# Attention scores from high and low parts in three products, and one group of block inverses turned a stage later

## What is computed

```python
q = partial_rope(rms_norm(q, g_q)) * d ** -0.5        # (B, T, 4 heads, 2 parts, d = 64)
k = partial_rope(rms_norm(k, g_k))
s = einsum('bqhcd,bkhcd->bhcqk', q, k)                # float32 scores, c = two parts
pr = softmax(s, axis=-1)
amap = pr[:, :, 0] - lam * pr[:, :, 1]
out = einsum('bhqk,bkhe->bqhe', amap, v)              # e = 128
```

## Time and profile before

| | us |
|---|---|
| median of 3 runs (lowest to highest) | 2118.28 (2113.72 to 2121.5) |
| the profiled execution | 2117.55 |
| its span, first to last instruction | 2115.7 |
| mean granted TensorE clock in it | 0.968 |

### The profile page before, as it was taken

How to read it: one execution, slowest core, us unless ns; L and a number is a source line. 1 busy time by engine, 2 the same in 40 slices (tenths; PEclk the granted TensorE clock), 3 DMA queues, 4 the chain that set the end, 5 groups by cost and what they waited for, 6 DMA issues and landing times. The chain is left out here.

```text
span 2115.7 us, 40868 instructions
## 1 busy us (share of the span) xinstructions
PE 1958.3 (93%) x16327; PEld 1657.1 (78%) x16327; DVE 1386.8 (66%) x2230; ACT 974.9 (46%) x1854; POOL 353.4 (17%) x354
## 2 busy tenths in 40 slices
PE   5999999999767888869999799999999999999999
PEld 4666777777665666658886688999999999988887
DVE  4877757675676668667777557755655556647566
ACT  7454458785564555534454323432333322343433
POOL 0000000000007999274463100000000000000000
PEclk9999999999788999879999999999999999999999
DMA  4111147786950000148983532222222222394343
GB/s 186 67 47 46 69 179 245 243 281 222 358 196 34 1 1 1 34 116 192 204 182 108 180 120 110 90 84 91 98 84 84 84 92 102 131 340 146 100 144 112
DMA packets 151867, 275.22 MB, mean 130 GB/s; under 512 B 12960, under 2 KB 85408, under 8 KB 149504
## 3 DMA queue, kind: packets, MB, share of 16 engines
q1 hardware_dynamic: 151392, 271.27, 39.9%
q10 hardware_dynamic: 288, 1.34, 0.2%
HBM read 169.67 MB, written 99.93 MB: 127 GB/s over the span
## 5 line engine op out<-in xcount | busy, mean ns | idle before, releaser
L222 PE MATMUL normed_acc<-right_t_high,normed_lefts 128*128 128x320 f32 x528 | 163.8, 310 | 3.8 <-DVE normed_lefts L3107 3.8
L224 PE MATMUL normed_acc<-right_t_high,normed_lefts 128*128 128x320 f32 x528 | 163.8, 310 | 0.0
L223 PE MATMUL normed_acc<-right_t_low,normed_lefts 128*128 128x320 f32 x528 | 163.8, 310 | 0.0
L3107 DVE TENSOR_TENSOR normed_lefts<-held_room,normed_lefts 128x512 fp32r<-128x512 f32 x149 | 102.3, 687 | 91.1 <-ACT normed_lefts L2993 91.1
L222 PE MATMUL normed_acc<-normed_nl 128*128 128x512 f32 x385 | 149.8, 389 | 0.0
L224 PE MATMUL normed_acc<-normed_nl,normed_nh 128*128 128x512 f32 x385 | 149.8, 389 | 0.0
L2993 ACT CAST normed_lefts<-held_room 128x512 fp32r<-128x512 f32 x149 | 90.4, 620 | 109.5 <-DMA held_room<-in_w_up 48.3
L3015 ACT COPY normed_n<-normed_acc 128x640 f32<-128x640 f32 x64 | 44.5, 695 | 206.5 <-PE normed_acc L224 203.5
L3179 DVE TENSOR_TENSOR normed_nl<-held_room,normed_nh 128x640 fp32r<-128x640 f32 x77 | 63.3, 823 | 91.7 <-ACT normed_nh L3041 91.6
L3041 ACT CAST normed_nh<-held_room 128x640 fp32r<-128x640 f32 x77 | 56.1, 728 | 143.8 <-PE normed_acc L224 124.6
L222 PE MATMUL pj_acc<-parts_nh,pj_w0rest 128*128 128x512 f32 (+1 forms) x288 | 110.1, 382 | 7.1 <-DVE parts_nl L804 7.1
(11 more groups left out here) (414 smaller groups left out, 5639.0 us busy)
## 6 DMA issues: line engine op xcount, KB each, us to landing
held_room<-dram_h SPq DMA_DIRECT2D x77, 320.0 KB, 3.0
dram_sx<-pr_sx SPq DMA_DIRECT2D x16, 1024.0 KB, 4.5
ch_ops<-dram_sx SPq DMA_DIRECT2D x56, 256.0 KB, 5.2
dram_h<-held_room SPq DMA_DIRECT2D x44, 320.0 KB, 2.3
pj_packed<-in_w_in SPq DMA_DIRECT2D x24, 512.0 KB, 4.9
heads_vt<-dram_ab SPq DMA_DIRECT2D x44, 256.0 KB, 7.1
held_room<-in_w_gate SPq DMA_DIRECT2D x22, 512.0 KB, 4.4
held_room<-in_w_up SPq DMA_DIRECT2D x22, 512.0 KB, 4.4
```

What stands on the lines that cost most here:

```text
L222: nc.tensor.matmul(out, ll, rh, start=start, stop=False, skip_group_check=onto_kept)
L223: nc.tensor.matmul(out, lh, rl, start=False, stop=False, skip_group_check=onto_kept)
L224: return nc.tensor.matmul(out, lh, rh, start=False, stop=stop, skip_group_check=onto_kept)
L3107: tt(lefts[:, q % LEFTS, 1, :], raw[:, y, QUARTER[p], :], lefts[:, q % LEFTS, 0, :].bitcast(F32), ALU.subtract).then_inc(low, 1)
```

## The change

The score product is no longer one float32 matmul. Queries and keys are split into a high part (a copy into the type fp32r, by ScalarE) and a low part (what is left, subtracted by VectorE), and each score piece is the sum of three fp32r matmuls: low query with high key, high query with low key, high with high. The keys of a head are split once, in two pieces (the short sequence's 272 columns, the long one's 1040); the queries are split for each unit, two units ahead, into two buffers. For heads 1 to 3 the short piece is split in unit i = 5 of the head before, the long piece in unit i = 0. On ScalarE the copies stand at the end of a step, behind `out_of`; on VectorE the subtractions stand behind `largest(k, 1)` and ahead of `turn_inverse`, each with a wait for the copy. TensorE waits for the low parts. The tiles of the stage are laid out anew, and ScalarE waits, ahead of its step 1, for the stores of the stage before. `EARLY` goes from 4 to 3.

```diff
@@ -1020,7 +1020,7 @@
     return (n % GS // 2 * 4 + x * 2 + n % 2) * FT + f
 
 
-PAIR, EARLY = 2, 4
+PAIR, EARLY = 2, 3
 
 
 def links_until(pair):
@@ -1916,11 +1916,13 @@
     ALL = len(units)
...
+        kh, kl = (c.sb(n, (P, TOK), F32R) for n in ("kh", "kl"))
+        qh, ql = ([c.sb(f"{n}{s}", (P, P), F32R) for s in range(2)] for n in ("qh", "ql"))
+        st = [c.sb(f"st{s}", (P, 2, 4)) for s in range(2)]
+        lams = c.sb("lams", (P, 4))
         pr = [[c.sb(f"pr{s}{x}", (P, LEN_B)) for x in range(2)] for s in range(2)]
         amT = [c.sb(f"amT{s}", (P, 9, P)) for s in range(2)]
-        st = [c.sb(f"st{s}", (P, 2, 4)) for s in range(2)]
         lam = g.lam
-        lams = c.sb("lams", (P, 4))
         solve_chain, first_in = c.sem("solve_chain"), c.sem("first_in")
         FIRST_TURN = ALL - 4 * EARLY
         pS = [c.ps(f"pS{x}", (P, 3 * 512)) for x in range(2)]
...
+        k_high, k_low, q_high, q_low = (c.sem(n) for n in ("k_high", "k_low", "q_high", "q_low"))
+        KEYS = (slice(0, LEN_A), slice(LEN_A, TOK))
+        SHORT = sum(u[3] == LEN_A for u in units[:NU])
+
+        def splits_behind(k):
+
+            h, i = k // NU, k % NU
+            return [(h + 1, 0)] if i == NU // 2 and h + 1 < HEADS else [(h, 1)] if i == 0 and h else []
 
         turned, act_copied = c.sem("turned"), c.sem("act_copied")
         tiles_of = [[range(0, 4), range(4, 8), range(8, 9)] if u[3] == LEN_B else [range(0, 3)] for u in units]
@@ -1961,13 +1971,16 @@
                     if k:
                         for x in range(2):
                             pe.wait_ge(exped[x], k)
+                    pe.wait_ge(q_low, k + 1)
+                    if k % NU in (0, SHORT):
+                        pe.wait_ge(k_low, 2 * h + (1 if k % NU == 0 else 2))
                     for lo in range(0, ln, 512):
                         hi = min(lo + 512, ln)
-                        for x, rows in enumerate(HALVES):
-                            last = mm(pS[x][:, lo:hi], g.qr[rows, h, q0:q0 + P], g.kr[rows, h, a + lo:a + hi],
-                                      start=True, stop=True)
-                            if hi == ln:
-                                last.then_inc(scores[x], 1)
+                        for n, (left, right) in enumerate(((ql, kh), (qh, kl), (qh, kh))):
+                            for x, rows in enumerate(HALVES):
+                                last = mm(pS[x][:, lo:hi], left[k % 2][rows, :], right[rows, a + lo:a + hi], start=n == 0, stop=n == 2)
+                                if hi == ln and n == 2:
+                                    last.then_inc(scores[x], 1)
 
                 def turn(k, b):
                     ln = units[k][3]
@@ -2027,12 +2040,32 @@
                         last = nc.scalar.copy(amT[k % 2][0:kn, full, :], pTail[0:kn, :] if b == 2 else pT[0:kn, full * P:(full + 1) * P])
                     last.then_inc(act_copied, 1)
 
+                def high_keys(h, part):
+                    if h:
+                        for x in range(2):
+                            act.wait_ge(scores[x], NU * (h - 1) + SHORT if part == 0 else NU * h)
+                    nc.scalar.copy(kh[:, KEYS[part]], g.kr[:, h, KEYS[part]]).then_inc(k_high, 1)
+
+                def high_queries(k):
+                    if k >= 2:
+                        for x in range(2):
+                            act.wait_ge(scores[x], k - 1)
+                    q0 = units[k][1]
+                    nc.scalar.copy(qh[k % 2][:, :], g.qr[:, units[k][0], q0:q0 + P]).then_inc(q_high, 1)
+
                 def out_of(k):
                     act.wait_ge(outs, k + 1)
                     nc.scalar.copy(g.o_rows[:, units[k][0], k % NU, :], pO[:, 0:P]).then_inc(ocopied, 1)
+                high_queries(0)
+                high_keys(0, 0)
+                high_queries(1)
+                high_keys(0, 1)
                 act.wait_ge(lamb, 1)
                 nc.scalar.activation(lams[:, 0:2], lams[:, 0:2], ACT.Exp).then_inc(lamb, 1)
                 for k in range(ALL + 2):
+                    if k == 1:
+                        for sem, n in g.solve_stored:
+                            act.wait_ge(sem, n)
                     if 1 <= k <= ALL:
                         turn_copy(k - 1, 0)
                     if k < ALL:
@@ -2043,6 +2076,11 @@
                             turn_copy(k - 1, b)
                     if k >= 2:
                         out_of(k - 2)
+                    if k < ALL:
+                        for h, part in splits_behind(k):
+                            high_keys(h, part)
+                    if k + 2 < ALL:
+                        high_queries(k + 2)
 
             @block.vector
             def _(dve):
@@ -2091,6 +2129,18 @@
                         nc.vector.transpose(g.by_row_early[:, grp, :, part].rearrange("p u c -> p c u"),
                                             g.inv[:, grp, :, part].rearrange("p i j -> p j i"))
 
+                def low_keys(h, part):
+                    dve.wait_ge(k_high, 2 * h + part + 1)
+                    nc.vector.tensor_tensor(kl[:, KEYS[part]], g.kr[:, h, KEYS[part]], kh[:, KEYS[part]].bitcast(F32), ALU.subtract).then_inc(k_low, 1)
+
+                def low_queries(k):
+                    q0 = units[k][1]
+                    dve.wait_ge(q_high, k + 1)
+                    nc.vector.tensor_tensor(ql[k % 2][:, :], g.qr[:, units[k][0], q0:q0 + P], qh[k % 2][:, :].bitcast(F32), ALU.subtract).then_inc(q_low, 1)
+                low_queries(0)
+                low_keys(0, 0)
+                low_queries(1)
+                low_keys(0, 1)
                 lambda_sums()
                 for k in range(ALL + 1):
                     if k:
@@ -2100,6 +2150,11 @@
                         largest(k, 1)
                     if k == 0:
                         lambdas()
+                    if k < ALL:
+                        for h, part in splits_behind(k):
+                            low_keys(h, part)
+                    if k + 2 < ALL:
+                        low_queries(k + 2)
                     if FIRST_TURN <= k < ALL:
                         turn_inverse(k - FIRST_TURN)
 
```

## The result

The changed kernel takes 2190.72 us (median of 4 runs, 2185.67 to 2196.69), the kernel before 2117.12 beside it: ratio 1.034, interval 1.0318 to 1.0363. The forecast was 2182, its range 2155 to 2214. The profiled execution took 2187.64 us (span 2185.9, mean clock 0.955). What follows is its trace.

What follows compares the result with a forecast made beforehand. The attention stage was taken as bound by a loop of score, maxima and exponential, 5.90 us long, hiding the difference with 0.31 to spare. Terms 24.2, 17.7, 2.3, 11.5, 6 and 3.2 added 64.9 to 2117.55: 2182 us, range 2155 to 2214.

Steps and rivals of the forecast that it cites:

- the difference no longer starts at E + 0.1 but after ScalarE's whole tail: Each unit's query split: VectorE's reciprocal and difference wait for ScalarE's query copy and its subtraction, held 1.25 us.
- E: In the attention stage, the moment when both exponentials of a unit are done; VectorE's reciprocal followed 0.1 us later.
- Ordinary steps: Long units after long units: 1.05 us more each, 23 times, 24.2 us; query subtraction of 128 columns taken as 0.28.
- Short keys: Units 5, 15, 25, where 272 key columns are split: 0.77 us each, 2.3 us in all.
- Long keys: Blocks around units 10, 20, 30, where 1040 key columns are split: 5.9 us each, 17.7 in all.
- Inverses: VectorE's inverse pieces, exposed whole between query wait and difference in ten steps: 1.15 us each, 11.5 in all.
- Clock: TensorE's clock falls after idle time in steps with exposed inverses: 6 us, between 0 and 15.
- Start: Attention stage's start, first score and exponential behind the first splits: unit 3 comes 3.2 us late (2 to 5).
- in ordinary units too: Rival: TensorE's clock falls also after the 1.4 us idle time of ordinary units, 34 us more: 2212 us; chance 0.11.
- halves apart: Rival: score halves run one after the other on TensorE, scores of 2.7 to 4 us: 2194 us; chance 0.09.
- The score decides: Rival: the query split costs the loop under 0.31 us, so only the shorter score counts: 2117 us; chance 0.04.
- four passes: Rival: three products against float32's four passes cut a quarter of 66 us of long scores: 2101 us; chance 0.02.

Runs made afterwards that it cites:

- experiment 4: Changed kernel with ScalarE's query copies moved from the end to the head of its step, ahead of the transposes' copy: 2149.52 us, ratio 1.015 against the kernel before.
- experiment 8: Changed kernel with ScalarE's query and key copies both moved to the head of its step: 2119.22 us, ratio 1.0003 against the kernel before.
- experiment 9: Changed kernel with VectorE's key and query subtractions moved behind the next step's difference, ScalarE's list unchanged: 2140.45 us, ratio 1.0105 against the kernel before.
- experiment 6: Changed kernel with GpSimd's substitution cut to one element per instruction, so block inverses are left out: 2175.44 us, ratio 1.0258 against the kernel before.
- experiment 7: Changed kernel with extra unused matmuls keeping TensorE busy ahead of its wait for the difference: 2181.09 us, ratio 1.0292 against the kernel before.
- experiment 1: Kernel before with only EARLY cut from 4 to 3, no splits: 2117.71 us, ratio 0.9998 against the kernel before.

## Why the prediction held

*What decides.* The step "the difference no longer starts at E + 0.1 but after ScalarE's whole tail" held. Experiments 4, 8 and 9 show it by taking the chain apart at either end. Without GpSimd in the way (experiment 6) maxima to reciprocal takes 4.95 us against 3.74 in the earlier trace rows, a hold of 1.21 where 1.25 was forecast; reciprocal to maxima is 1.72 against 2.16, so 0.44 came back where I gave 0.31.

*Ordinary steps, right for partly wrong reasons.* The 12 periods of the first three heads without key split, inverse or a step right behind short keys' fall average 7.01, 1.11 over 5.90, where 1.05 was forecast. But without GpSimd (experiment 6) eleven of them are 6.66 to 6.69, 0.77 over; the twelfth, right behind a step with short keys, is 8.30. The step that failed is "0.28 for 128": that rate is from the earlier trace rows, where GpSimd rests, and beside it the subtraction takes 0.56. I saw the effect in the wide pass and did not carry it to the new instructions.

*Short keys, the worst term.* "0.77 each", 2.3 in all. Over 7.01 the three steps are 2.45, 2.82 and 0.55 longer, and the first is followed by one 3.13 longer: 9.0. In experiment 6 all three are 7.14, 0.5 over an ordinary one, and the last is followed by the 8.30. The rest is GpSimd, and the clock: the rows of step 5 have 3.88 us of idle TensorE, then four transposes in 1.11 instead of 0.66 and a values product of 4.34 instead of 2.36. I had counted slow matmuls for inverses and long keys, and had ordinary steps as a rival, but none for the short keys.

*Long keys.* "5.9, with 4 and 8 as ends" was too low. The blocks cost 8.5, 10.0 and, after four inverses at 0.95 (next term), 7.6: 26.1 against 17.7. The followed order was right, the steps longer. Timeline of the changed kernel's first such block, where E of unit 9 is 713.3 (the first line's end; the last two lines end at E of units 12 and 13):

```profile
713.09 0.21 ACT L2026 ACTIVATION_READ_ACCUMULATOR at_pr<-at_pS,at_st 128x1 f32 x1
...
720.97 1.05 ACT L2047 CAST at_kh<-heads_kr 128x1040 fp32r<-128x1040 f32 x1
...
721.93 0.29 ACT L2054 CAST at_qh<-heads_qr 128x128 fp32r<-128x128 f32 x1
...
722.06 1.26 DVE L2134 TENSOR_TENSOR at_kl<-heads_kr,at_kh 128x1040 fp32r<-128x1040 f32 x1 [4.71 <-ACT at_kh L2047]
...
723.25 0.93 DVE L2139 TENSOR_TENSOR at_ql<-heads_qr,at_qh 128x128 fp32r<-128x128 f32 x1
...
725.45 0.90 PE L1995 MATMUL at_pT<-at_ident,at_pr 128*128 128x128 f32 x3 [4.62 <-DVE at_pr L2117]
...
726.14 3.49 PE L2006 MATMUL at_pO<-heads_vt,at_amT 128*128 128x128 f32 x18
...
729.83 0.30 ACT L2054 CAST at_qh<-heads_qr 128x128 fp32r<-128x128 f32 x1
...
735.33 0.19 ACT L2026 ACTIVATION_READ_ACCUMULATOR at_pr<-at_pS,at_st 128x1 f32 x1
...
742.40 0.19 ACT L2026 ACTIVATION_READ_ACCUMULATOR at_pr<-at_pS,at_st 128x1 f32 x1
```

The key copy starts at E + 7.7 (forecast 7.4) and takes 1.05 (1.07), its subtraction 1.26 (1.25). The query subtraction takes 0.93 (0.28), and `times_v(9)` ends at 16.3 (16.1). E of unit 12 is at 22.2 (21.8); unit 13's score then runs at the lower clock (records 0.43 us apart), and its E is at 29.3 (28.0). With TensorE kept busy the second and third block are 2.5 and 1.9 us shorter, the first is not.

*Inverses.* 1.15 each was forecast; steps with one take 7.58 to 7.71 where the clock holds, 0.95 over the 6.67 of a step that GpSimd leaves alone (experiment 6). A little less than forecast, and exposed whole, as forecast.

*Clock.* 6 forecast, 8.1 measured by experiment 7, though only in part where I had put it: with TensorE kept busy units 3 to 9 and 19 to 23, which have key splits, are 2.5 us shorter each, and 33 to 39, with inverses, 2.75. In the changed kernel idle times of 1.2 to 1.7 us in ordinary steps were not followed by a fall, so the rival "in ordinary units too" is out; in experiment 6 one of 1.64, in a step with short keys, was.

*Start.* 3.2 forecast, 4.6 found; with the copies moved 2.5 stays.

*Covered edits.* The third late group and the moved copies of the next stage cost nothing (experiment 1), as forecast; that the next stage even gets 2.7 us shorter was not, and why was not looked into.

*The other rivals.* The six wide steps of the score start 0.23 us apart, both halves side by side, its first and last record 1.6 us apart, and the last ends 1.89 after the first began: forecast 1.7; the rival of halves apart is out. "The score decides" and "four passes" needed a difference that is not held; experiment 8 shows that even a freed score of three products does not make this kernel faster while GpSimd works. Nor is it a quarter shorter: 1.89 from the first record to the last one's end stand against 2.12 in the earlier trace rows.

So the sum of 64.9 missed 8.2 of the stage's 73.1. GpSimd's long instructions beside VectorE's are worth 15.4 there, of which the forecast had only 0.1 a unit; it was partly made up by ordinary steps that are 0.28 cheaper without it than I had put them, and by inverses that are 0.2 cheaper. That these errors run against each other, and the total comes so near, is luck; that the difference is held, and by about 1.2 us, is not.

## What to carry to other kernels

On engines that work in order, a copy appended to one list and its consumer appended to another make a chain through both tails. Ask for every new wait what is queued behind it, and put both ends where their engines are idle anyway: here that is worth 70 us with no instruction saved. Take the price of a two-operand instruction of VectorE from rows in which GpSimd works as it will at the new place.

## What the runs showed of the hardware beyond that

In the rows read, a VectorE instruction with two operands in SBUF (the tiles that the kernel allocates with `c.sb`; PSUM, `c.ps`, holds what TensorE writes) that meets a running GpSimd instruction ends only after that one has ended: 1.37 us for 272 columns against 0.44 with short GpSimd instructions, 1.25 against 0.29 for 128 columns. It goes the other way too. GpSimd's addition over 504 columns took 2.05 us beside the wide pass, and ended 1.03 after it; one over 510 columns took 1.18 beside the maxima (at 677.22):

```profile
683.97 1.65 DVE L2117 SCALAR_TENSOR_TENSOR at_pr<-at_pr,at_st 128x1040 f32<-128x1040 f32 x1
...
684.60 2.05 POOL L1047 TENSOR_TENSOR held_room<-held_room,solved_solve_tmp 128x504 f32<-128x504 f32 x1
```

The Trainium skill, "SBUF — State Buffer", section "SBUF: two separate sides", says that VectorE and GpSimd share a pair of ports as an exclusive lock, held for a whole instruction, which a VectorE instruction with two SBUF inputs needs when the GpSimd one reads SBUF. The rows agree: in step 5 the subtractions are delayed by 0.93 and 0.96 us, with 1.07 and 1.11 left of the GpSimd instruction. What experiment 6 shows by itself is that the length of GpSimd's instructions sets the delay. The maxima, with their one operand from PSUM, took 2.38 and 2.39 in either kernel.
